# Refilling a place of rounded weights one product sooner in the attention stages

## What is computed

```
q, k, v, ..., qm = split(x @ w_in[j])           # A also has the indexer's columns
mix = attention of the layer's kind(rope(q), rope(k), v)     # 12 heads of 64
mo  = memory_attention(qm, mk, mv)                           # 4 heads, 256 memory rows
mixed = concat(mix, mo) @ w_out[i]
x = layer_norm(ALPHA * x + mixed, ln1_g[i], ln1_b[i])
x = layer_norm(ALPHA * x + swiglu(x, w_gate_up[i], w_down[i]), ln2_g[i], ln2_b[i])
```

## Time and profile before

| | before |
|---|---|
| median of 3 runs | 1554.36 us (1553.69 to 1554.85) |
| the profiled execution | 1553.68 us, its span 1551.9 us |
| TensorE matmul queue busy | 98% of the span |
| DVE busy | 70% |
| ACT busy | 49% |
| granted TensorE clock, mean | 0.999 |

### The profile page before, as it was taken

One profiled execution on the slowest core, in us unless ns is written; L12 is line 12 of the kernel. 1 busy time (PEld: TensorE's weight loads), 2 busy tenths in 40 slices (PEclk: granted clock), 3 DMA queues, 4 the chain that ended last, 5 costly groups with the idle time before them and its releaser, 6 DMA issues.

```text
span 1551.9 us, 19840 instructions
## 1 busy us (share of the span) xinstructions
PE 1528.5 (98%) x8091; PEld 1267.8 (82%) x8091; DVE 1088.2 (70%) x1561; ACT 760.7 (49%) x963; POOL 52.1 (3%) x89
## 2 busy tenths in 40 slices
PE   9999999999999999999999999999999999999997
PEld 7887788888878888888788888877888888978986
DVE  6986866656777775676966756888667678567764
ACT  5657444444445443346544343566444434574463
POOL 1100000000000000000000000000100000000010
PEclk9999999999999999999999999999999999999999
DMA  8661666644435766352476654533766645433530
GB/s 320 245 231 55 226 224 264 249 174 179 163 104 201 262 261 243 138 215 83 178 252 234 244 225 148 204 109 136 267 257 236 223 166 223 164 118 140 217 122 27
DMA packets 45898, 299.87 MB, mean 193 GB/s; under 512 B 5540, under 2 KB 5796, under 8 KB 12528
## 3 DMA queue, kind: packets, MB, share of 16 engines
q1 hardware_dynamic: 39600, 278.74, 48.6%
q0 software_dynamic: 5776, 19.01, 3.7%
q10 hardware_dynamic: 432, 0.85, 0.1%
HBM read 296.20 MB, written 2.65 MB: 193 GB/s over the span
## 4 chain that ended last, share of the span: by engine, by line
PE 83%; DVE 9%; ACT 4%; issue 2%; DMA 0%; POOL 0%; POOLq 0%; SPq 0%; DVEq 0%; ACTq 0%
PE psum L1309 53%; PE psum L1268 15%; PE psum L1303 7%; DVE w_low L1777 3%; PE psum L1163 2%; PE psum L1238 1%; PE psum L1422 1%; ACT work L1604 1%; PE psum L1325 1%; ACT w_high L1528 1%; PE psum L1306 1%; DVE work L2061 1%; PE psum L1376 1%; DVE work L2099 1%; DVE xt_low L1811 0%
## 5 line engine op out<-in xcount | busy, mean ns | idle before, releaser
L1528 ACT ACTIVATE w_high<-w_raw 128x2048 fp32r<-128x2048 f32 (+1 forms) x240 | 456.4, 1903 | 230.7 <-DMA w_raw<-in_weights 144.9
L1777 DVE TENSOR_TENSOR w_low<-w_raw,w_high 128x2048 fp32r<-128x2048 f32 (+2 forms) x240 | 530.0, 2214 | 34.4 <-ACT w_high L1528 33.3
L1309 PE MATMUL psum<-w_high,xt_high 128*128 128x512 f32 (+1 forms) x1376 | 378.6, 395 | 1.4 <-DVE x_rows L1875 0.7
L1309 PE MATMUL psum<-w_high,xt_low 128*128 128x512 f32 (+1 forms) x1376 | 368.4, 388 | 0.3 <-DVE xt_low L1811 0.3
L1309 PE MATMUL psum<-w_low,xt_high 128*128 128x512 f32 (+1 forms) x1376 | 368.1, 388 | 0.0
L1309 PEld LDWEIGHTS psum<-w_high,xt_low 128*128 128x128 f32 x1376 | 257.4, 188 | 54.8 <-DVE xt_low L1811 0.7
L1309 PEld LDWEIGHTS psum<-w_low,xt_high 128*128 128x128 f32 x1376 | 257.3, 188 | 53.7 <-DVE w_low L1777 0.4
L1309 PEld LDWEIGHTS psum<-w_high,xt_high 128*128 128x128 f32 x1376 | 249.8, 188 | 52.5 <-DVE x_rows L1875 2.3
L2128 DVE TENSOR_TENSOR arena<-arena,psum 128x256 f32<-128x256 f32 x88 | 36.9, 420 | 205.4 <-ACT arena L1663 205.0
L1663 ACT ACTIVATE arena<-psum 128x256 f32<-128x256 f32 x88 | 33.7, 383 | 218.5 <-PE psum L1309 218.5
L1268 PE MATMUL psum<-w_high,ht_high 128*128 128x512 f32 x352 | 99.9, 401 | 0.0
(11 more groups left out here) (253 smaller groups left out, 1494.8 us busy)
## 6 DMA issues: line engine op xcount, KB each, us to landing
w_raw<-in_weights SPq DMA_DIRECT2D x260, 1024.0 KB, 4.8
norm_params<-in_ln_g POOLq DMA_DIRECT2D x8, 512.0 KB, 4.4
norm_params<-in_ln_b POOLq DMA_DIRECT2D x8, 512.0 KB, 5.9
w_raw<-in_weights SPq DMA_DIRECT2D x4, 656.0 KB, 6.1
kv_outside<-arena POOLq DMA_DIRECT2D x3, 512.0 KB, 4.5
mem_kv<-kv_outside POOLq DMA_DIRECT2D x3, 512.0 KB, 3.7
norm_params<-mods_outside POOLq DMA_DIRECT2D x3, 512.0 KB, 5.8
x_rows<-in_x SPq DMA_DIRECT2D x4, 256.0 KB, 5.6
```

The lines of the kernel that those rows point to most:

```text
L1309: m = e.matmul(psum[:, bank, 0:w], rows[:, kk, rb * P:rb * P + P], right[:, at:at + w], start=first, stop=last)
L1528: e.activation(K.w_hi[:, g % RING, 0:w], K.w_raw[:, r, 0:w], ACT.Copy).then_inc(K.high.hit(t), 1)
L1777: m = e.tensor_tensor(K.w_lo[:, s, 0:n], K.w_raw[:, r, 0:n], K.w_hi[:, s, 0:n].bitcast(F32), ALU.subtract)
```

## The change

In `some` the products hand `prompt=True` to `gemm`. A tile that has had its second product there is counted as owed at once, and the next `split` or `ahead` rounds the next tile into its place, where it would have done so one call later. `some` is called in the attention stages of the four layers, in each for the values and the memory queries; the products for the keys before it and for `w_out` behind it had `prompt` already. No instruction is added or left out.

```
         def some(n, tiles, where, sort, hooks):
             use = self.gemms.take()
             for half in range(2):
-                self.gemm(tiles[half], n, half, gen, "gemm", use, sort)
+                self.gemm(tiles[half], n, half, gen, "gemm", use, sort, prompt=True)
                 if half:
                     by = ("dve",) * 2 if where[0] == "qm" else ("act",) * 2 if where == ("proj", LAST, 3) else ("act", "dve")
                     self.evacuate(where, by=by)(n, use, tiles[half])
                 hooks[half]()
```

## The result

| | before | after |
|---|---|---|
| median of 14 runs each, side by side | 1553.88 us (1553.52 to 1555.52) | 1558.24 us (1556.27 to 1561.42) |
| ratio | | 1.0028, 95% interval 1.0020 to 1.0036 |
| the profiled execution, its span | 1553.68 us, 1551.9 us | 1556.40 us, 1554.6 us |

The changed kernel is slower by 4.4 us. Its profiled execution is only 2.7 us longer, and it is one of its shortest. The executions of after spread over 5 us, those of before over 2, and a longer one has as a rule a lower mean granted clock of TensorE: 1556.40 us at 0.999, 1558.95 us at 0.996, 1561.20 us at 0.995. So there are two things to explain: the part that the trace shows, and the part that comes and goes.

The account below looks back on a forecast made before the run. TensorE, its matmul queue 98% busy, was taken as the bound. Layer terms of -0.4, +1.5, +0.2 and +1.4 sum to +2.7 us, giving 1557.0 us on the median of 1554.36; the forecast's own range is 1555.8 to 1558.4.

Parts of the forecast that it names:

- What bounds the kernel: TensorE's matmul queue, busy 98%; sooner weights gain nothing, the change acts only through the ACT and DVE queues.
- The new places: First new rounding: in layer 0 behind `mix_split` on ACT, in layers 1 to 3 ahead of the ACT copy L1560.
- The three losses: TensorE's `weigh` waits for copy L1560 behind a rounding: layer 1 +1.5, layer 2 +0.7, layer 3 +1.8 us.
- The gains: Waits that go: for L1648 at layer 2's last place, -0.5 us; for L1875 in layers 0 and 3, -0.5 each.
- The sum: Layer 0 -0.4, layer 1 +1.5, layer 2 +0.2, layer 3 +1.4 us; together +2.7.
- Rivals 1 to 3: 1: delays taken back, 1553.9, chance 0.14; 2: halved subtractions uncovered, 1559.2 to 1561.4, chance 0.14; 3: nothing moves, 1554.4, chance 0.06.
- Rival 4: TensorE's clock falls to 1.2 GHz at three new gaps, 2.8 us each, +8.4 on the sum: 1565.4; chance 0.02.

Follow-up runs that it names:

- layer 3 alone: The kernel before with `prompt` added in layer 3 only: median 3.1 us over before, ratio 1.0016.
- the filled kernel: The changed kernel with 11, 4 and 14 unread transposes on TensorE in the new gaps of layers 1, 2 and 3: 1556.01 us, ratio 1.0011 to before.
- the pure delay: The kernel before with 17 unread transposes on TensorE at the place of the changed kernel's layer 1 gap: 1555.46 us, ratio 1.0013 to before.

## Why the prediction was right, and where it was short

The forecast was 1557.0 us, within 0.2% of before or just past it; measured is 1558.24, ratio 1.0028: within the range, but past the line. The kernel before has a median of 1554.36 in the forecast and 1553.88 side by side, so the change is +4.4 where +2.7 was forecast. That this still lies inside the forecast's own range (up to 1558.4) is partly luck: some 1.7 of it is a term that the sum didn't have. By its steps:

- **What bounds the kernel** held: the weights come sooner and TensorE gains nothing from that; all of the effect came by the queues of ACT and DVE.
- **The new places** are as worked out: in layers 1 to 3 L1528 stands directly ahead of L1560, and in layer 0 the ACT rounding blocks no copy.
- **The three losses.** Forecast 1.5, 0.7 and 1.8; the marks on the matmul queue are 1.48, 0.58 and 1.84. The 0.31 of the earlier trace rows is a mark of the weight-load queue, and there the longest wait for L1560 is now 2.1, which is 1.8 more. The row of 1.80 us from a rounding's start to the next start gave the price in all three.
- **The gains.** The wait for L1648 at the last place of layer 2 is gone, and so is the wait for L1875 in layers 0 and 3 on the matmul queue. Layer 0 gave 0.4 to 0.6 (forecast 0.4).
- **The sum.** Forecast +2.7; shown by the profiles +2.2, +2.4 and +2.7. No term is off by clearly more than such shifts can tell: layer 2 is 0.0 instead of +0.2, layer 3 between 1.0 (alone) and 1.9 instead of 1.4.
- **Rivals 1 to 3** are refuted: the waits behind the gaps kept their size (L2117 in layer 1 is 1.7 us in after as in before), no wait for L2099 came on, and the order and the times did move.
- **Rival 4** is the step that failed. I had it as all or nothing: three falls in every execution, 2.8 us each, +8.4, chance 0.02. In truth a fall costs 1.3 to 1.6 us and comes in some executions: four in the four profiles of after, and +1.7 over before by the mean clocks, as coarse as these are. The forecast's sum should have held it as a term. My argument against it was one stretch of the one profile of before, where a stretch with little matmul was granted 1.00; but after's first profile has three new gaps with a clock of 1.00 too, and the next executions don't. One profile can't exclude what happens in a part of the executions. The clocks of many executions can show it, even where they differ only in the third decimal: 0.001 of this span is 1.6 us.

The part shown by the trace and the part by the clock make 2.2 to 2.7 + 1.7 = 3.9 to 4.4, against 4.4 and 3.6 measured in two sets of runs. With the uncertainty of both parts that is an agreement, not a proof of the second.

The Trainium skill, TensorE: Matmul & The Clock Gate, Part 1: The HAM clock gate, says that the default is the throttled state and activity releases it, and that the gate's look at the activity runs freely and doesn't begin with the kernel, so that the same program differs from run to run. The four profiles of one kernel (0, 1, 2 and 1 falls) agree with this. Which execution meets it where was not controlled here, so it is no more than an agreement. The prediction took from that section that a fall would need longer gaps than these; the falls behind idle marks of 1.47 and 1.86 us decide against that.

**Open.** What decides where the clock falls isn't settled. The length of one gap alone doesn't: the old wait of 1.7 us for L2117 in layer 1 stands in all 14 profiles, and the clock falls behind it in none. The two waits for L2185 stand in before too, and its one profile has no fall there. Of the six profiles with the new gap of layer 3 open three have a fall there (two of after, and layer 3 alone), of the eight others none; in the filled kernel both waits are as long as ever (1.08 and 0.73 us), and none of its 11 executions has a clock of 0.997 or less. That speaks for a part of layer 3's gap in these falls too, but how it would reach some 240 us further isn't shown. The other reading, that the moment matters, is as open: the three falls come where the first L2185 starts at 1287.8 to 1288.3, and the pure delay reached 1287.0. Filling the old waits missed them.

## What to carry to other kernels

Before an operation is moved forward in an in-order queue, look at what stands behind its new place and who waits for that: here 1.90 us of rounding that nobody needed yet went ahead of 0.57 us of copy that the busiest engine needed at once. Put the copy on the other engine, or the rounding behind it; here the first brought back the time of before (ratio 0.9999), and no more. A gap on TensorE costs its own length and can cost, in some executions, a slower clock behind it; compare the granted clocks of several executions, not one profile, before you call that cost zero.

## What was not expected of the hardware

- The clock fell to half (1.2 GHz) behind new gaps of 1.5 to 1.9 us, and behind two waits of 1.08 and 0.73 us with four transposes between them, in some executions and not in others of the same program; each fall cost 1.3 to 1.6 us. Behind an old gap of 1.7 us it fell in none of 14 profiles.
- Transposes that nothing reads, in the place of idleness, kept the mean clock at 0.9985 instead of 0.9971, and the median was 2.2 us lower, of which 0.3 to 0.8 is a shorter delay, though they do no work.
- The clock falls to half at the end of every profile, when TensorE has nothing left to do. A mean granted clock over the span therefore holds 1.6 to 2.9 us that slow no matmul.
- Profiles of kernels that are the same up to there differ by up to 2.3 us at 140 us of the span (140.27 to 142.53 for the same ACT instruction). What a change does is therefore better read from shifts along the span than from two spans.
